# Six output tiles and a query GEMM around the second norm, one tile behind the first turn, and first passes on a constant

## The chip, the cores and the metric

The kernel runs on one core of a Trainium2 chip. The metric is the device time of one execution in microseconds (us), median of three.

## What is computed

One block of a hybrid network on 256 tokens of width 1024, all in float32. A mixer (a sparse attention of 8 heads and a gated recurrence of 4 heads) ends in the product with w_out; then come a residual and a layer norm. A cross attention of 4 heads over 256 memory rows ends in the product with xa_wo; then the second residual and norm. Last come product-key experts: a query for 8 heads, the best 16 of 128 by 128 keys for each, a product of all tokens with the 16384 rows of down, a gelu, the gates, and a product with the 16384 rows of up; then the third residual and norm. Cut to what matters here:

```python
mix = _hybrid_mixer(x, ...)                       # ends in @ w_out
x = _layer_norm(DEEPNORM_ALPHA * x + mix, ln_g[l, 0], ln_b[l, 0])
xa = _memory_cross_attention(x, mem, ...)         # ends in o @ wo
x = _layer_norm(DEEPNORM_ALPHA * x + xa, ln_g[l, 1], ln_b[l, 1])
qry = (t @ wq).reshape(T, PEER_HEADS, 2, PEER_DKEY // 2)
s = jnp.einsum('thcd,hcnd->thcn', qry, sub_keys)
s1, i1 = lax.top_k(s[:, :, 0], PEER_TOPK)
```

## The kernel before

All large weights come as a stream of tiles of 128 by 1024 numbers (512 KB), loaded by SP's queue into eight raw slots, for the expert tables into five. Every product is made at near float32 precision with two rounded numbers per operand: ACT copies a raw tile into `hi` (`split`, L600), DVE or, for tiles POOL_FROM to POOL_TO, POOL subtracts it from the raw tile into `lo`, in the raw tile's place (`rest`, L800; POOL's at L586), and PE makes three products (`three`, L1254 to L1256): hi by hi, hi by lo, lo by hi. There are four `hi` slots, so tile n + 4 is split when tile n is used (semaphore tile_used).

Tiles have two kinds. A column tile (T) holds 128 output columns for all 1024 input rows: 8 blocks of k, 24 products of 256 columns, and the result stands transposed, feature by token. A row tile (R) of width 512 holds two blocks of k: 6 products of 512 columns for each of two token tiles of 128 tokens (t = 0 and 1), 12 in all, and the result stands token by feature. A matrix of 1024 columns is 8 tiles of either kind. `plan` (L49) lists them, `order` (L126) writes one list, ORDER, of steps by hand, and every engine walks it and does its own part of each step, in order. The names that matter:

- `gemm`: PE's products with a tile; ACT takes a finished column result out of psG and splits tile n + 4, DVE makes the remainder. `feed` and `feed_lo` are the split and the remainder alone.
- `joint`: the last three output tiles, all of them for t = 0 first and then for t = 1, so that the norm of t = 0 can begin.
- `norm`: DVE adds the residual (`add_residual`, L817), takes the statistics, and normalizes in two halves of 512 columns (`normalize`, L832 and L838); ACT takes the root (L751).
- `turn`: PE transposes 128 tokens (L1549), ACT copies the result rounded into o_hi or b_hi (L757), DVE the remainder into o_lo or b_lo (`turn_lo`, L1125). Turns 0 and 1 are of the recurrence's output (four transposes each, ahead of the third tile of w_out, and `gemm` waits for o_lo at its first product), turns 2 and 3 of the first norm, 4 and 5 of the second, for t = 0 and 1.
- `route`: PE scores one head of the query against the keys, two products (L1526), ACT copies the scores out (L742), and DVE searches (`route`, L955 to L986): 8-wide maxima, index searches, replacements, and a sum of all 16 by 16 pairs (L967).

Around the second norm ORDER is: the cross attention's stages with ten stream tiles between them (the last two are output tiles), three more output tiles, `joint` of three, the norm of t = 0 and t = 1, turns 4 and 5, and then the eight column tiles of the query, a `route` behind each from the second on. Then the down table begins, a column tile for every 128 experts (`down`); DVE, which is then still searching, makes remainders again from table tile 24 on.

At the start SP loads x in four parts and tile 0 in two halves between them, then tiles 1, 2 and 3 whole; ACT splits x (L684) and tile 0 (L688) by parts, DVE makes the remainders (L936, L941), and PE's first product waits for them.

## Time and profile before

| | |
|---|---|
| median of 3 runs | 1080.71 us (1078.92 to 1081.68) |
| the profiled execution | 1080.01 us, span 1077.9 us |
| PE busy | 1051.9 us (98%) |
| DVE, ACT, POOL busy | 765.5, 513.5, 83.8 us |
| mean granted TensorE clock | 0.993 |

The profile shows one execution: for each engine its instructions with start and duration, what an idle time ended with, and the clock granted to TensorE in a stretch. Products are pipelined, so their pace is read from start to start, not from the duration of one. "Idle before" with an arrow names the instruction that released the engine.

### The profile page before, as it was taken

The page shows a single profiled execution, that of the slowest core. Times are in us where ns is not written, and L with a number is a line of the kernel's source. Part 1 is how long each engine was busy: PE and PEld are TensorE (multiplying, and loading weights), DVE is VectorE, ACT ScalarE, POOL GpSimd, SP SyncE. Part 2 cuts the span into 40 slices and gives each one's busy share as a digit, 9 for nine tenths or more (in the row PEclk, how much of TensorE's full clock was granted, in tenths as well). Part 3 has the DMA queues.
Part 4 walks back from the last instruction along what each step waited for, and adds up shares of the span by engine and source line. Part 5 has one row for each costly group of instructions (what it writes and reads, how often), then busy time and mean ns, then how long its engine had stood idle before and what let it go on. Part 6 is the DMA issues. An engine that isn't in the chain of part 4 may idle for free.

```text
span 1077.9 us, 18835 instructions
## 1 busy us (share of the span) xinstructions
PE 1051.9 (98%) x7648; PEld 949.2 (88%) x7648; DVE 765.5 (71%) x1431; ACT 513.5 (48%) x806; POOL 83.8 (8%) x57
## 2 busy tenths in 40 slices
PE   7999999999899999999999999999999999999996
PEld 6987887898799999999999999988888888888885
DVE  4667766845799876446888885488889885555556
ACT  5554544454455555544444444544444444554542
POOL 3000000000268700000000000000000000000000
PEclk9999999999899999999999999999999999999999
DMA  9843234643335555555544545565555555665652
GB/s 328 338 163 98 99 118 135 240 136 118 98 118 177 185 187 178 179 187 176 163 157 159 169 162 176 177 215 176 176 169 170 173 173 195 195 192 190 191 192 94
DMA packets 51589, 186.61 MB, mean 173 GB/s; under 512 B 5936, under 2 KB 5984, under 8 KB 51120
## 3 DMA queue, kind: packets, MB, share of 16 engines
q1 hardware_dynamic: 49680, 178.80, 50.7%
q0 software_dynamic: 1824, 6.61, 1.8%
q8 instruction: 61, 1.00, 0.4%
q14 instruction: 24, 0.20, 0.1%
HBM read 183.82 MB, written 1.05 MB: 172 GB/s over the span
## 4 chain that ended last, share of the span: by engine, by line
PE 95%; DVE 3%; DMA 1%; ACT 1%; issue 0%; SPq 0%; ACTq 0%
PE psG L1254 17%; PE psG L1255 17%; PE psG L1256 17%; PE psS L1606 16%; PE psT L1606 16%; PE psO L1574 2%; PE psO L1575 1%; PE psO L1501 1%; DMA raw<-in_w_stream 1%; PE psS L1413 1%; PE psO L1436 1%; PE psS L1357 1%; DVE x L838 1%; PE psS L1254 1%; PE psS L1256 1%; PE psS L1255 1%
## 5 line engine op out<-in xcount | busy, mean ns | idle before, releaser
L800 DVE TENSOR_TENSOR lo<-raw,hi 128x1024 fp32r<-128x1024 f32 x302 | 368.3, 1221 | 152.7 <-ACT hi L600 152.6
L600 ACT ACTIVATE hi<-raw 128x1024 fp32r<-128x1024 f32 x330 | 349.1, 1059 | 264.9 <-DMA raw<-in_up 188.1
L1254 PE MATMUL psG<-b_hi,hi 128*128 128x256 f32 x1152 | 332.2, 288 | 1.6 <-DVE b_lo L1125 1.2
L1255 PE MATMUL psG<-b_lo,hi 128*128 128x256 f32 x1152 | 327.2, 284 | 0.0
L1256 PE MATMUL psG<-b_hi,lo 128*128 128x256 f32 x1152 | 327.1, 284 | 0.0
L1254 PEld LDWEIGHTS psG<-b_hi,hi 128*128 128x128 f32 x1152 | 222.3, 193 | 3.7 <-issue 3.4
L1255 PEld LDWEIGHTS psG<-b_lo,hi 128*128 128x128 f32 x1152 | 222.4, 193 | 0.2
L1256 PEld LDWEIGHTS psG<-b_hi,lo 128*128 128x128 f32 x1152 | 222.2, 193 | 0.0
L766 ACT ACTIVATE H<-psG 128x256 f32<-128x256 f32 x128 | 49.1, 383 | 174.5 <-PE psG L1256 174.5
L1232 DVE TENSOR_TENSOR act_lo<-H,act_hi 128x256 fp32r<-128x256 f32 x128 | 54.0, 424 | 98.2 <-ACT act_hi L784 98.0
L1606 PE MATMUL psS<-hi,act_hi 128*128 128x512 f32 x248 | 79.5, 401 | 0.0
L586 POOL TENSOR_TENSOR lo<-raw,hi 128x1024 fp32r<-128x1024 f32 x28 | 69.6, 2491 | 97.3 <-ACT hi L600 97.3
L1606 PE MATMUL psT<-lo,act_hi 128*128 128x512 f32 x248 | 76.8, 391 | 0.0
L1606 PE MATMUL psT<-hi,act_hi 128*128 128x512 f32 x248 | 76.8, 391 | 0.0
L1606 PE MATMUL psS<-lo,act_hi 128*128 128x512 f32 x248 | 76.7, 391 | 0.0
L1606 PE MATMUL psS<-hi,act_lo 128*128 128x512 f32 x248 | 76.6, 390 | 0.0
L1606 PE MATMUL psT<-hi,act_lo 128*128 128x512 f32 x248 | 76.6, 390 | 0.0
L1254 PE MATMUL psG<-o_hi,hi 128*128 128x256 f32 x192 | 57.5, 300 | 8.1 <-DVE lo L941 7.2
L1255 PE MATMUL psG<-o_lo,hi 128*128 128x256 f32 x192 | 55.7, 290 | 0.0
L1256 PE MATMUL psG<-o_hi,lo 128*128 128x256 f32 x192 | 55.6, 290 | 0.0
L1606 PEld LDWEIGHTS psT<-hi,act_lo 128*128 128x128 f32 x248 | 46.6, 188 | 10.1
L1606 PEld LDWEIGHTS psT<-lo,act_hi 128*128 128x128 f32 x248 | 46.6, 188 | 10.1
(320 smaller groups left out, 1439.7 us busy)
## 6 DMA issues: line engine op xcount, KB each, us to landing
raw<-in_down SPq DMA_DIRECT2D x128, 512.0 KB, 3.5
raw<-in_up SPq DMA_DIRECT2D x128, 512.0 KB, 3.5
raw<-in_w_stream SPq DMA_DIRECT2D x74, 512.0 KB, 3.6
w<-in_w SPq DMA_DIRECT2D x4, 512.0 KB, 11.5
xT<-in_xT SPq DMA_DIRECT2D x4, 256.0 KB, 5.6
memT<-in_memT SPq DMA_DIRECT2D x1, 1024.0 KB, 8.1
x_tok<-in_x_tok POOLq DMA_DIRECT2D x1, 1024.0 KB, 8.6
ln_gb<-in_ln_g POOLq DMA_DIRECT2D x2, 512.0 KB, 6.9
```

Of the source, the lines that this page charges most:

```text
L586: pool.tensor_tensor(lo[slot(n)][:], raw[slot(n)][:], hi[n % DEPTH][:].bitcast(FP32), ALU.subtract)\
L600: act.activation(hi[n % DEPTH][:], raw[slot(n)][:], ACT.Copy).then_inc(hi_done, 1)
L766: act.activation(H[:, j, :], psG[j % 2][:, 0:S], ACT.Gelu).then_inc(h_out, 1)
L800: dve.tensor_tensor(lo[slot(n)][:], raw[slot(n)][:], hi[n % DEPTH][:].bitcast(FP32), ALU.subtract)\
L838: dve.scalar_tensor_tensor(out=z[:, half], in0=z[:, half], scalar=rs[:, t, 0:1], in1=gb[:, 1, half], op0=ALU.mult, op1=ALU.add).then_inc(r ...
L1232: dve.tensor_tensor(a_lo[j % 4][:], H[:, j, :], a_hi[j % 4][:].bitcast(FP32), ALU.subtract)\
L1254: pe.matmul(out, hi_l, hi_r, start=start, stop=False)
L1255: pe.matmul(out, hi_l, lo_r, start=False, stop=False)
L1256: return pe.matmul(out, lo_l, hi_r, start=False, stop=stop)
L1357: pe.matmul(psS[:, at:at + keys], qT[group * HD:(group + 1) * HD, 2 * g + j, t * P:(t + 1) * P], kT[b][group * HD:(group + 1) * HD, 0:keys ...
L1574: pe.matmul(out[:, k, :], one2[s][:, k // 2, :, k % 2], one1_hi[s][:, k // 2, :, k % 2], start=True, stop=False)
L1606: mm = pe.matmul((psS, psT)[t][:, c * 512:(c + 1) * 512], left[:, cut], right[:, c * 512:(c + 1) * 512], start=st, stop=False)
```

## The change

- **The start.** DVE sets a small bf16 array to one, and PE makes 28 products of 256 columns with it (WARM) into psT, whose result nothing reads, before the first real product. Tile 1 is loaded, split and subtracted in two halves, as tile 0 is.
- **The first turn.** The tiles of w_out come in another order: (0, 0), (0, 2), then the first tile of the second half (1, 0), then (0, 4), (0, 6) and the joint three. The turns stand ahead of the third tile as before, which is now (1, 0). Turns 0 and 1 write to psG, turns 2 and 5 to psT, 3 and 4 to psO.
- **The second norm.** Six output tiles (CROSS_JOINT) are made for t = 0 first; then four of them for t = 1, turn 4, and the other two for t = 1. The query of the first four heads is made of four row tiles, for t = 0 ahead of turn 5 and for t = 1 behind it. ACT copies its two banks to `probs`, PE transposes them (8 transposes) to psT, and ACT copies them to qryT. Four column tiles for the other heads follow, with one, two, two and three `route` steps behind them.
- **Slots.** Output and query tiles also use four more `hi` slots in the place of o_hi and o_lo, which are free by then. POOL makes the remainders from the third query tile on (before, from the fifth).

```diff
-        ("xo", "R", 0, 2), ("pq", "T", 0, KD)]
...
-CROSS_TILES = [(0, 0), (1, 0), (0, 2), (0, 4), (0, 6), (1, 2), (1, 4), (1, 6)]
-JOINT = 3
+        ("xo", "R", 0, 2), ("pq", "R", 0, 1), ("pq", "T", 4, 4)]
...
+OUTPUT_TILES = {"wo": [(0, 0), (0, 2), (1, 0), (0, 4), (0, 6), (1, 2), (1, 4), (1, 6)],
+                "xo": [(0, 0), (1, 0), (0, 2), (0, 4), (0, 6), (1, 2), (1, 4), (1, 6)]}
+JOINT, CROSS_JOINT = 3, 6
...
+FIRST, WARM = 2, 28
...
-    gemm(AT["pq"] - JOINT - n)
-    joint = range(n, n + JOINT)
-    n += JOINT
-    out += [("joint", joint[0]), ("norm", (1, 0))] + [("feed", m) for m in joint]
-    out += [("norm", (1, 1)), ("turn", 4), ("turn", 5), ("turn_lo", 4), ("turn_lo", 5)] + [("feed_lo", m) for m in joint]
+    assert n == AT["pq"] - CROSS_JOINT
+    joint = range(n, n + CROSS_JOINT)
+    n += CROSS_JOINT
+    out += [("part", (m, 0)) for m in joint]
+    out += [("feed", m) for m in joint[:4]] + [("feed_lo", m) for m in joint[:4]] + [("norm", (1, 0))]
+    out += [("part", (m, 1)) for m in joint[:4]] + [("feed", m) for m in joint[4:]]
+    out += [("turn", 4), ("half", 1), ("turn_lo", 4)] + [("part", (m, 1)) for m in joint[4:]]
+    query = range(n, n + 4)
+    n += 4
+    out += [("feed", query[0]), ("feed", query[1]), ("norm", (1, 1))] + [("part", (m, 0)) for m in query]
+    out += [("turn", 5), ("turn_lo", 5), ("query", 0), ("feed", query[2]), ("feed", query[3])]
+    out += [("part", (m, 1)) for m in query] + [("query", 1), ("turn_query", 0), ("turn_query", 1)]
     gemm(1)
-    for h in range(PH):
-        gemm(min(1, N1 - n))
-        out.append(("route", h))
+    out += [("route", 0)]
+    gemm(1)
+    out += [("route", 1), ("route", 2)]
+    gemm(1)
+    out += [("route", 3), ("route", 4)]
+    gemm(1)
+    out += [("route", h) for h in range(5, PH)]
     return out
...
-POOL_FROM, POOL_TO = N1 - 4, N1 + 24
+POOL_FROM, POOL_TO = N1 - 6, N1 + 24
...
+def hi_slot(n):
+
+    q = (n - AT["xo"]) % (2 * DEPTH)
+    if AT["xo"] <= n < N1 and q >= DEPTH:
+        return q
+    return n % DEPTH
...
+        held[hi_slot(n)] = n
...
+        o_at = place["at"]
         o_hi = sb("o_hi", [P, KD, S], F32R)
         o_lo = sb("o_lo", [P, KD, S], F32R)
+        hi += [sb(f"hi{DEPTH + i}", [P, D], F32R, at=o_at + i * D * 4) for i in range(DEPTH)]
         ln_gb = sb("ln_gb", [P, 2, D])
...
+        warm_in = sb("warm_in", [P, S], BF16, at=place["at"])
...
+        def turned_out(i, b):
+
+            return psG[i][:] if i < 2 else turned_bank(i)[:, b * 512:(b + 1) * 512]
+
+        def turned_bank(i):
+
+            return psT if i in (2, 5) else psO
...
-            for n in range(1, ALL):
+            for n in range(1, FIRST):
+                for c in range(2):
+                    half = slice(c * D // 2, (c + 1) * D // 2)
+                    sp.dma_start(raw[n][:, half], a["w_stream"][n][:, half]).then_inc(first_in[2 * n + c], 16)
+            for n in range(FIRST, ALL):
...
+                elif what == "query":
+                    if i == 0:
+                        act.wait_ge(query_done, 1)
+                        act.wait_ge(cross_turned, XH)
+                    else:
+                        act.wait_ge(tile_used, AT["pq"] + 4)
+                    act.activation(probs[:, i * 512:(i + 1) * 512], bank[BANK[TILES[AT["pq"]][8] + i]], ACT.Copy)\
+                        .then_inc(act_took, 1)
+                elif what == "turn_query":
+                    act.wait_ge(query_turned, i + 1)
+                    act.activation(qryT[:, 0:4, i * P:(i + 1) * P],
+                                   psT[:, i * 512:(i + 1) * 512].rearrange("p (k c) -> p k c", c=P), ACT.Copy)\
+                        .then_inc(query_ready, 1)
...
+            dve.memset(warm_in[:], 1.0).then_inc(warm_ready, 1)
...
+            for n in range(1, FIRST):
+                for c in range(2):
+                    half = slice(c * D // 2, (c + 1) * D // 2)
+                    dve.wait_ge((first_hi, hi_done)[c], n + 1)
+                    dve.tensor_tensor(lo[n][:, half], raw[n][:, half], hi[n][:, half].bitcast(FP32), ALU.subtract)\
+                        .then_inc((first_lo, lo_done)[c], 1)
...
+                elif what == "half":
+                    add_residual(FIRST_HALVES[2], (i,))
                 elif what == "norm":
                     w, t = i
-                    add_residual((AT["wo"] + KD, AT["pq"])[w] - 1, (t,))
+                    for n in FIRST_HALVES[2 * w:2 * w + 2]:
+                        if n >= (AT["wo"] + KD, AT["pq"])[w] - (JOINT, CROSS_JOINT)[w] and (w, t, n) != (1, 1, FIRST_HALVES[2]):
+                            add_residual(n, (t,))
...
+            def part(n, t):
+
+                name, kind, i, k0, m, cols, first, last, use = TILES[n]
+                lo_wait(n)
+                if name == "xo":
+                    pe.wait_ge(cross_lo, k0 // 2 + 1)
+                if name == "pq" and k0 % 4 == 0:
+                    pe.wait_ge(turn_lo, TURNED[4 + t] - 1 + k0 // 4)
+                if name == "pq" and k0 == 0:
+                    pe.wait_ge(dve_took, TAKEN[BEFORE[use + t]][1])
+                for kk in range(m):
+                    cut = slice(kk * cols, (kk + 1) * cols)
+                    k = k0 + kk
+                    left_hi, left_lo = (o_hi, o_lo) if name == "wo" else (b_hi, b_lo)
+                    mm = three(bank[BANK[use + t]], left_hi[:, k, t * P:(t + 1) * P],
+                               left_lo[:, k, t * P:(t + 1) * P], hi[hi_slot(n)][:, cut], lo[slot(n)][:, cut],
+                               k == 0, k == KD - 1)
+                if t == NT - 1:
+                    mm.then_inc(tile_used, 1)
+                elif last:
+                    mm.then_inc(query_done if name == "pq" else first_half, 1)
...
+            pe.wait_ge(warm_ready, 1)
+            for i in range(WARM):
+                pe.matmul(psT[:, 0:S], warm_in[:, 0:P], warm_in[:], start=True, stop=True)
             for what, i in ORDER:
                 if what in ("gemm", "bare"):
                     gemm(i)
                 elif what == "joint":
-                    joint(i)
+                    for t in range(NT):
+                        for m in range(i, i + JOINT):
+                            part(m, t)
+                elif what == "part":
+                    part(*i)
+                elif what == "turn_query":
+                    pe.wait_ge(act_took, TAKEN[TILES[AT["pq"]][8] + i][1])
+                    pe.wait_ge(turn_lo, TURNED[5])
+                    for h in range(4):
+                        mm = pe.transpose(psT[:, i * 512 + h * P:i * 512 + (h + 1) * P],
+                                          probs[:, i * 512 + h * P:i * 512 + (h + 1) * P], ident[:])
+                    mm.then_inc(query_turned, 1)
...
-                    pe.wait_ge(act_took, TAKEN[TILES[AT["pq"] + i][8]][1])
+                    if i < 4:
+                        pe.wait_ge(query_ready, NT)
+                    else:
+                        pe.wait_ge(act_took, TAKEN[TILES[AT["pq"] + i][8]][1])
...
                     if i == 0:
-                        pe.wait_ge(exp_done, XU)
-                        pe.wait_ge(probsT_ready, XU)
+                        pe.wait_ge(act_took, TAKEN[TILES[AT["mv"]][8] + 1][1])
                     elif i in (2, 3):
...
                         if i < 2:
-                            src = oh[:, t, k % 4 * P:(k % 4 + 1) * P]
+                            src, out = oh[:, t, k % 4 * P:(k % 4 + 1) * P], psG[t][:, k % 4 * P:(k % 4 + 1) * P]
                         else:
                             src = (x1, x2)[i // 2 - 1][:, t, k * P:(k + 1) * P]
-                        mm = pe.transpose((psO if i in (2, 4) else (psS, psT)[t])[:, k * P:(k + 1) * P], src, ident[:])
+                            out = turned_bank(i)[:, k * P:(k + 1) * P]
+                        mm = pe.transpose(out, src, ident[:])
                         if k % 4 == 3:
```

How the order moves. PE at the first turn, of the kernel before (`oh` is the recurrence's output, `p_hi` and `o_hi` the left operands of w_out's first and later rows, psO and psS the banks of its first and second half):

```order
L1256 MATMUL psO<-hi_54,o_lo 128x512
L1549 MATMUL psS<-ident,oh 128x128 x4
L1549 MATMUL psT<-ident,oh 128x128 x4
L1254 MATMUL psO<-hi_55,o_hi 128x512
L1255 MATMUL psO<-lo_61,o_hi 128x512
```

and of the change:

```order
L1333 MATMUL psO<-lo_59,o_hi 128x512
L1334 MATMUL psO<-hi_54,o_lo 128x512
L1648 MATMUL psG<-ident,oh 128x128 x8
L1332 MATMUL psS<-hi_55,p_hi 128x512
L1333 MATMUL psS<-lo_61,p_hi 128x512
L1334 MATMUL psS<-hi_55,p_lo 128x512
```

Behind the transposes stood products with o_hi, which the turn writes; now 12 products with p_hi and p_lo stand there first. ACT at the second norm, of the kernel before (from the root of t = 0 to the first query result; `hi` from `raw` is a split):

```order
L751 ACTIVATE std<-mv 128x1
L600 ACTIVATE hi_54<-raw_66 128x1024
L600 ACTIVATE hi_55<-raw_107 128x1024
L600 ACTIVATE hi_56<-raw_109 128x1024
L751 ACTIVATE std<-mv 128x1
L757 ACTIVATE b_hi<-psO 128x4x128 x2
L757 ACTIVATE b_hi<-psT 128x4x128 x2
L617 ACTIVATE qryT<-psG 128x256
```

and of the change:

```order
L820 ACTIVATE std<-mv 128x1
L653 ACTIVATE hi_55<-raw_107 128x1024
L653 ACTIVATE hi_56<-raw_109 128x1024
L826 ACTIVATE b_hi<-psO 128x4x128 x2
L653 ACTIVATE hi_115<-raw_111 128x1024
L653 ACTIVATE hi_116<-raw_58 128x1024
L820 ACTIVATE std<-mv 128x1
L826 ACTIVATE b_hi<-psT 128x4x128 x2
L787 ACTIVATE probs<-psG 128x512
L653 ACTIVATE hi_117<-raw_60 128x1024
L653 ACTIVATE hi_118<-raw_62 128x1024
L787 ACTIVATE probs<-psG 128x512
```

Both turns stood behind both roots; now turn 4 stands between them, with two splits ahead of it, and two more splits stand ahead of the root of t = 1.

## Rows read from the trace of the kernel before

**Rows 1.** page, section 1, the whole span
```profile
PE 1051.9 (98%) x7648; PEld 949.2 (88%) x7648; DVE 765.5 (71%) x1431; ACT 513.5 (48%) x806; POOL 83.8 (8%) x57
```

**Rows 2.** what PE waited for, whole span: us in total, times, longest
```profile
PE psG L1254 <- DVE lo L941: 7.2, 2, 6.6
...
PE psT L1549 <- DVE x L838: 3.4, 2, 2.6
...
PE psO L1254 <- DVE o_lo L1125: 2.3, 1, 2.3
...
PE psG L1254 <- DVE b_lo L1125: 1.2, 1, 1.2
```

**Rows 3.** busy time by stretch, granted TensorE clock last but two
```profile
0.00:15.40 15.40, 8.01 (x33) 7.20 (x34) 6.98 (x9) 8.39 (x11) 5.48 (x13) 1.00 0.84 303
...
179.00:182.60 3.60, 3.60 (x10) 2.81 (x9) 0.13 (x1) 0.00 (x0) 0.00 (x0) 0.53 0.00 0
...
279.50:285.00 5.50, 5.48 (x26) 5.50 (x27) 3.87 (x4) 0.00 (x0) 0.00 (x0) 0.50 0.00 0
```

**Rows 4.** order of time, the first tiles: start us, us, engine, instruction [idle before]
```profile
12.27 3.77 DVE L800 TENSOR_TENSOR lo<-raw,hi 128x1024 fp32r<-128x1024 f32 x3 [1.34 <-ACT hi L600]
...
12.45 1.06 ACT L600 ACTIVATE hi<-raw 128x1024 fp32r<-128x1024 f32 x1 [0.22 <-DMA raw<-in_w_stream]
...
13.55 0.58 PE L1254 MATMUL psG<-o_hi,hi 128*128 128x256 f32 x1 [0.24 <-DVE lo L800]
...
14.78 0.41 PE L1256 MATMUL psG<-o_hi,lo 128*128 128x256 f32 x1
...
14.99 0.41 PE L1254 MATMUL psG<-o_hi,hi 128*128 128x256 f32 x1
...
15.51 0.28 PE L1254 MATMUL psG<-o_hi,hi 128*128 128x256 f32 x1
...
15.63 0.28 PE L1255 MATMUL psG<-o_lo,hi 128*128 128x256 f32 x1
```

**Rows 5.** order of time, PE after the first turn
```profile
179.66 0.63 PE L1254 MATMUL psO<-hi,o_hi 128*128 128x512 f32 x1
...
180.08 0.63 PE L1255 MATMUL psO<-lo,o_hi 128*128 128x512 f32 x1
```

**Rows 6.** order of time, PE and DVE at the second norm
```profile
271.23 0.39 PE L1254 MATMUL psS<-hi,b_hi 128*128 128x512 f32 x1
...
271.46 0.39 PE L1255 MATMUL psS<-lo,b_hi 128*128 128x512 f32 x1
...
272.77 0.68 DVE L817 SCALAR_TENSOR_TENSOR x<-x,psS 128x512 f32<-128x512 f32 x1
...
277.63 0.66 PE L1549 MATMUL psT<-ident,x 128*128 128x128 f32 x4 [0.80 <-DVE x L838]
```

**Rows 7.** page, sections 5 and 6: POOL's remainders, loads of the stream
```profile
L586 POOL TENSOR_TENSOR lo<-raw,hi 128x1024 fp32r<-128x1024 f32 x28 | 69.6, 2491 | 97.3 <-ACT hi L600 97.3
...
raw<-in_w_stream SPq DMA_DIRECT2D x74, 512.0 KB, 3.6
```

**Rows 8.** the stream's loads in the first 20 us
```profile
DMA to landing us min/median/max: 7.6/11.5/16.6
```

**Rows 9.** order of time, scoring, search and tile 24
```profile
287.74 1.03 PE L1526 MATMUL psO<-subk,qryT 128*128 128x256 f32 x4
...
289.92 1.06 DVE L955 MAX8 unit_m<-route_s 128x8 f32<-128x128 f32 x4 [6.54 <-ACT route_s L742]
...
311.72 0.47 PE L1254 MATMUL psG<-b_hi,hi 128*128 128x256 f32 x1
...
343.03 2.58 DVE L967 TENSOR_TENSOR unit_c<-unit_m 128x256 f32<-128x256 f32 x2
...
353.88 0.74 DVE L967 TENSOR_TENSOR unit_c<-unit_m 128x256 f32<-128x256 f32 x2
...
374.35 1.34 DVE L800 TENSOR_TENSOR lo<-raw,hi 128x1024 fp32r<-128x1024 f32 x1 [2.01 <-ACT hi L600]
```

More of the change, by code:

```diff
@@ L245, with hi_slots @@
 SLOT_BEFORE, ARRIVED = slots()
+def hi_slot(n):
[3 more added lines that the diff above has]
+    return n % DEPTH
+def hi_slots():
+    held, before = {q: AT["xo"] - 1 for q in range(DEPTH, 2 * DEPTH)}, []
+    for n in range(ALL):
+        before.append(held.get(hi_slot(n)))
+        held[hi_slot(n)] = n
+    return before
+HI_BEFORE = hi_slots()
 def table_order():
@@ L466, in build @@
         x_in = [sem(f"x_in{i}") for i in range(4)]
-        first_in = [sem(f"first_in{i}") for i in range(2)]
+        first_in = [sem(f"first_in{i}") for i in range(2 * FIRST)]
+        warm_ready = sem("warm_ready")
         first_hi, first_lo = sem("first_hi"), sem("first_lo")
@@ L597, in split @@
                 act.wait_ge(raw_in[slot(n)], ARRIVED[n])
[L598 to L600 removed]
+                if HI_BEFORE[n] is not None:
+                    act.wait_ge(tile_used, HI_BEFORE[n] + 1)
+                act.activation(hi[hi_slot(n)][:], raw[slot(n)][:], ACT.Copy).then_inc(hi_done, 1)
             def take(n):
@@ L689, in _ @@
                         .then_inc((first_hi, hi_done)[i // 2], 1)
-            for n in range(1, DEPTH):
+            for n in range(1, FIRST):
+                for c in range(2):
+                    half = slice(c * D // 2, (c + 1) * D // 2)
+                    act.wait_ge(first_in[2 * n + c], 16)
+                    act.activation(hi[n][:, half], raw[n][:, half], ACT.Copy).then_inc((first_hi, hi_done)[c], 1)
+            for n in range(FIRST, DEPTH):
                 split(n)
```

78 lines of the change are left out of this document (31 added, 47 removed).

## The prediction

> **What bounds the kernel now.** I read first the busy shares: PE is busy for 98% of the span [rows 1], so only what lengthens or empties PE counts: its idle time, and passes that take longer than they need. The list of PE's waits came second. Four entries hold 14.1 of PE's idle time [rows 2]: 7.2 us for the first remainders of the weights, 3.4 us for normalized rows and 1.2 us for b_lo (both at the second norm), 2.3 us for o_lo at the first turn. Third I looked at the pace of the products. With 256 columns they follow each other by 0.12 us, but until 15.4 us by 0.21 us [rows 4]; with 512 columns by 0.227 us [rows 6], but behind the first turn by 0.42 us [rows 5]. The granted clock explains it: 0.53 in 179.0 to 182.6 us and 0.50 in 279.5 to 285.0 us, the level of 1.2 GHz in place of 2.4 [rows 3]. Each time PE had run a few transposes and waited before. For the first 15.4 us the column shows 1.00, but the step of 0.21 us is that of the 1.2 GHz stretches; there I go by the step. So three places cost PE twice, by a wait and by a slow clock behind it, and the change touches exactly these three. Last comes what lies behind: the search for experts on DVE, between 289.92 us and the remainder of table tile 24 at 374.35 us [rows 9], without a pause.
>
> **The start.** Added: a memset on DVE, 28 passes of 256 columns on a constant, and halves for tile 1 (one load, one ACT and one DVE instruction more, each of half size). At the slow step the passes take 28 x 0.213 = 6.0 us; PE is otherwise idle until 6.6 us [rows 2], so begun near 1 us they end near 7.0 us at worst. No trace shows bf16 passes here, so I bound them: at 0.12 us each they are over by 4.4 us, and if each took the 0.41 us that a slow one lasts in the rows [rows 4], they would end at 12.5 us and push the rest. I take the step of the fp32r passes with as many columns. What is won is read at tile 2: before, tile 1 starts at 13.55 us, makes 8 products at 0.21 and 16 at 0.12 us, and tile 2 starts at 17.2 us. With the fast level all along, tiles 0 and 1 no longer bound: the raw data of tile 2 arrive at 12.45 us, ACT takes 1.06 us, DVE 1.26 us (a third of 3.77) [rows 4], so tile 2 starts at 14.8 to 15.0 us. Gain 2.2 us; bounds 2.4 (nothing but that chain) and minus 1.1 (passes of 0.41 us). The halves of tile 1 alone, at a slow clock, give 0.5 us, since tile 1 then follows tile 0 without the pause before 13.55 us. Later tiles had slack: PE does not wait for a tile between 15.4 us and the turn, so the gain stays.
>
> **The first turn.** The output tile (1, 0) of 12 products, 12 x 0.227 = 2.7 us, comes between the transposes and the tile that needs o_lo. It uses only p_hi, p_lo and a weight tile already split; the transposes go to psG, which ACT has emptied by then. ACT and DVE do the same work in the same order behind the transposes, so o_lo is ready as before, 2.3 us behind them, and 2.7 us cover it. The wait of 2.3 us goes [rows 2]; the 3.6 us at a granted 0.53 [rows 3] shrink by 1.7 us, if the clock stays up while PE works. Gain 4.0 us. What moves: the residual of the first half comes one tile later on DVE, 2.7 us of work beside 4.1 us of joint products (18 x 0.227); it stays hidden. Bounds: 2.3 (the clock falls all the same) and 4.0.
>
> **The second norm.** On PE's own clock of before, the last six output tiles start at 271.9 - 72 x 0.227 = 255.6 us, and all their products for token tile 0 are done at 263.8 us in place of 267.8 us. DVE needs 5.0 us from there to the last normalized half (272.77 us is where it took up token tile 1 behind it [rows 6]), so x2 is ready near 268.8 us, while PE works on token tile 1 until 269.2 us. The turn of token tile 0 thus needs no wait. Behind it PE has 12 products (2.7 us) before the query GEMM, which covers ACT's and DVE's copies. But ACT now stands with two weight splits ahead of these copies, whose loads are issued only when parts for token tile 1 have freed slots, at 265 and 266.5 us; with 3.6 us to landing [rows 7] the second split ends at 271.1 us, b_lo at 272.6 us, PE arrives at 272.8 us: just covered. Then 24 products on token tile 0 (5.4 us, to 278.2 us) hide the norm of token tile 1, which DVE ends at 278.0 us. Only the turn of token tile 1 is open: before, its last transposes (0.66 us [rows 6]) and the wait for b_lo (1.2 us [rows 2]) took 1.9 us together; now eight transposes (1.0 us) run in these 1.9 us, which leaves 0.9 to 1.0 us idle. So of 3.4 + 1.2 us and a further 0.4 us at the first transposes, 1.0 remains: 4.0 us won. A new wait of 0.35 us arises between the two transposed query banks (a copy of 512 columns on ACT), and 8 transposes cost 1.0 us. Four query tiles as 48 products of 0.227 us in place of 96 of 0.12 us save 0.6 us. The stretch of 5.5 us at 0.50 [rows 3] becomes 3.0 us if the clock holds: 2.4 us (25 products at 0.213 in place of 0.12). Scoring comes in pairs behind column tiles, so PE changes between kinds of product five times in place of nine, 0.5 us. Together 4.0 - 0.35 - 1.0 + 0.6 + 2.4 + 0.5 = 6.2 us. Bounds: 3.8 (clock falls in the one idle place) and 7.2 (the turn needs no wait).
>
> **What is late next.** The search on DVE does not move as far as PE. Counted as above, token tile 1 of the query ends at 285.6 us, the transposed queries are there at 286.9 us, and the first column tile ends at 290.0 us in place of 287.74 us; the search follows by 2.2 us [rows 9]. It starts 2.3 us later, while PE's table tiles start 6.2 us earlier. Before, DVE was free 2.0 us before its remainder of tile 24 (374.35 us less the 2.01 us that it waited) and could have had it by 373.7 us; PE needs it at 311.72 + 24 x 2.88 + 0.2 = 381.0 us. The slack of 7.3 us meets a shift of 8.5 us: PE waits 1.2 us. Tiles before 24, and two query tiles more than before, come from POOL at 2.49 us each [rows 7] against 2.88 us of PE; that holds. Sum: 2.2 + 4.0 + 6.2 - 1.2 = **11.2 us** off the profiled 1080.0 us, 1068.8 us. The median of the runs shown is 0.7 us above that execution: **1069.5 us**.
>
> **Rivals.** (a) The first passes lose the fast level again, because PE has little to do between 7 and 10.4 us; for it speaks that idle stretches of 2 to 3 us ended in a slow clock twice [rows 3], against it that these pauses are shorter. The start gives 0.5 us, the time is 1071.2 us. Chance 0.17. (b) The search takes longer. A pair of sums at L967 takes 0.74 us or, beside a POOL subtraction, 2.58 us [rows 9]; over the eight heads such delays make 5.0 us. If five more of the eight were caught, at 1.84 us each 9.2 us, PE would wait 10.4 us: 1078.7 us; with two more, 1073.2 us. Chance of at least one and a half more 0.17. The Trainium skill ("SBUF — State Buffer", section "Who interferes with whom") says that a DVE instruction with two SBUF inputs and a GpSimd instruction reading SBUF exclude each other for a whole instruction; by that rule all eight pairs can be caught, and the search would be longer by 8 x 1.84 - 5.0 = 9.7 us in place of the unchanged length that I take. The trace agrees in the two lengths of the pair. (c) On the other side, slower: the loads behind the six tiles land late, and ACT, which works in order, holds the copies of the turn behind them. At 3.6 us to landing it costs nothing; each us above is a us of PE's wait at the query GEMM, and a slow stretch of 2.4 us follows. In the first 20 us, with many loads queued, landing took 7.6 to 16.6 us [rows 8]. At 11.5 us the loss is 10.3 us, which leaves 2.1 of 12.4 us (DVE is late as well, so tile 24 then costs nothing), 1078.6 us; slower than before from 13.6 us on, and 1083.7 us at 16.6 us. Against it: here only the weight stream loads. Chance 0.03. (d) The clock falls behind the turns all the same: 2.2 + 2.3 + 3.8 = 8.3 us, tile 24 then without a wait, 1072.4 us; the same that (a) has for and against it holds here. Chance 0.10.
>
> **How the numbers follow.** The forecast keeps 0.53. The range of 1066.8 to 1074.0 us runs from no wait at tile 24 and a little more from the turn, through (a), (d) and the nearer part of (b); the far part of (b) and (c) are left out. 0.3% is 3.2 us, about what a measurement of this kernel can tell from no change; faster than 1077.5 us are the forecast, (a), (d) and most of (b): 0.93. Within 0.3%: the far end of (b) and the mild case of (c), 0.05. Slower: 0.02.
>
> **What would show it.** Right: products 0.12 us apart from about 7 us on, tile 2 near 15 us; no wait for o_lo; the one wait behind the last turn near 1 us; no stretch at a granted 0.5 near either norm; table tile 0 starting near 299.3 us; one PE wait of about 1 us for DVE's lo near 368 us, since the search then ends last. Wrong: a slow step between 7 and 15 us (a); a wait of several us at tile 24 (b); PE waiting for b_lo before the query GEMM, with ACT waiting for the stream's loads (c).

## The result and the profile after

| | before | changed |
|---|---|---|
| median, same chip | 1080.69 us (4 runs) | 1073.44 us (4 runs: 1072.74 to 1077.50) |
| ratio of the times | 1 | 0.9949, 95% interval 0.9930 to 0.9969 |
| the profiled execution | 1080.01 us, span 1077.9 | 1077.50 us, span 1075.2 |

The change is faster, but by half of what was forecast: 0.51% by the ratio, 5.5 us of 1080 (by the interval 3.3 to 7.6), where 11.2 us were worked out. The two medians, of four runs each, lie 7.3 us apart; in the longer series of the same kernel (e1_after, below: five runs beside eleven) they lie 5.2 us apart, with a ratio of 0.9947 (0.9934 to 0.9960). What follows goes by the ratios. The profiled execution happens to be the slowest of the four; the second profile shows what is common to both.

First the page and PE's waits, as in [rows 1] and [rows 2] (us in total, times, longest). The change shifts line numbers: L1332 to L1334 are the products now, L653 the split, L668 `take`, L868 the remainder, L885 the residual, L900 and L906 the two normalize instructions, L1042 the search's sums of pairs, L1200 `turn_lo`, L1648 the transposes (one more each where the order list grew by a line, as in e2_pool).

```profile
PE 1054.6 (98%) x7636; PEld 947.6 (88%) x7636; DVE 762.6 (71%) x1431; ACT 514.1 (48%) x807; POOL 88.6 (8%) x59
```

```profile
PE psG L1332 <- ACT qT L668: 3.1, 2, 2.5
...
PE psT L1648 <- DVE x L906: 2.4, 2, 1.6
...
PE psG L1332 <- DVE lo L1010: 1.4, 1, 1.4
```

The wait for o_lo is gone, as forecast. The waits for `lo` fell from 7.2 to 1.4 us; 6.1 us of that stretch are now the constant passes, which are counted as busy. A new one stands on top: 3.1 us for ACT's copy of a finished product (qT), and the wait for normalized rows only fell from 3.4 to 2.4 us.

Busy time by stretch; the granted clock is the last column but two [rows 3]:

```profile
0.00:15.40 15.40, 12.48 (x76) 10.21 (x76) 7.23 (x11) 8.71 (x12) 5.47 (x13) 1.00 0.85 301
...
31.00:34.40 3.40, 3.40 (x19) 3.40 (x18) 2.26 (x2) 1.27 (x3) 0.00 (x0) 0.51 0.69 276
...
178.00:204.00 26.00, 26.00 (x125) 21.67 (x123) 20.98 (x31) 11.66 (x15) 0.65 (x2) 1.00 0.56 178
...
280.20:283.70 3.50, 3.44 (x10) 2.89 (x11) 1.31 (x2) 2.29 (x4) 0.18 (x1) 0.51 0.00 0
```

Nothing slow is left between the first turns and turn 3. But two stretches run low, and neither is in the forecast's sum: one behind the new wait for qT, one behind turn 5 (part of rival (d)).

The start, in order of time (start us, us, engine, instruction [idle before]), to be read with [rows 4]:

```profile
1.19 6.14 PE L1525 MATMUL psT<-warm_in 128*128 128x256 bf16 x28 [1.19 <-DVE warm_in L1001]
...
7.00 0.45 PE L1332 MATMUL psG<-o_hi,hi 128*128 128x256 f32 x1
...
15.50 0.35 PE L1332 MATMUL psG<-o_hi,hi 128*128 128x256 f32 x1 [0.39 <-ACT kvc L668]
...
28.27 1.06 ACT L653 ACTIVATE hi<-raw 128x1024 fp32r<-128x1024 f32 x1 [5.47 <-DMA raw<-in_w_stream]
...
29.23 0.36 ACT L668 ACTIVATE qT<-psG 128x256 f32<-128x256 f32 x1
...
29.74 0.36 PE L1332 MATMUL psG<-o_hi,hi 128*128 128x256 f32 x1 [2.50 <-ACT qT L668]
```

The constant passes end where forecast, the first real product follows at 7.00 us, and tile 2 starts at 15.50 us (before: 17.30). So 1.8 us were won by then. Then ACT stands 5.5 us for the load of tile 7. Its copy of tile 4's result is queued behind that split, and PE, which needs the bank, waits 2.5 us and from 31 us runs slow for 3 us. The transposes of turns 0 and 1 begin at 177.84 us; before, at 175.36.

The second norm, to be read with [rows 6]:

```profile
267.50 1.04 PE L1648 MATMUL psO<-ident,x 128*128 128x128 f32 x8
...
268.32 9.88 POOL L639 TENSOR_TENSOR lo<-raw,hi 128x1024 fp32r<-128x1024 f32 x4 [62.34 <-ACT hi L653]
...
270.73 1.29 DVE L1200 TENSOR_TENSOR b_lo<-psO,b_hi 128x512 fp32r<-128x512 f32 x2 [2.33 <-ACT b_hi L826]
...
271.93 0.68 DVE L885 SCALAR_TENSOR_TENSOR x<-x,psS 128x512 f32<-128x512 f32 x1
...
273.69 2.29 DVE L900 SCALAR_TENSOR_TENSOR x<-x,mv,ln_gb 128x512 f32<-128x512 f32 x1
...
276.08 2.67 DVE L906 SCALAR_TENSOR_TENSOR x<-x,rstd,ln_gb 128x512 f32<-128x512 f32 x1
...
278.68 0.74 DVE L900 SCALAR_TENSOR_TENSOR x<-x,mv,ln_gb 128x512 f32<-128x512 f32 x1
...
278.81 0.66 PE L1648 MATMUL psT<-ident,x 128*128 128x128 f32 x4 [1.58 <-DVE x L906]
...
281.60 0.63 PE L1333 MATMUL psG<-lo,b_hi 128*128 128x512 f32 x1
...
282.02 0.63 PE L1334 MATMUL psG<-hi,b_lo 128*128 128x512 f32 x1
```

Turn 4 comes without a wait. POOL begins on a query tile's remainder at 268.32 us and makes four in one go, to 278.20. While it runs, DVE's first two normalize instructions of token tile 1 (L900, L906) last 2.29 and 2.67 us, the third, behind it, 0.74. Beside POOL, too, but with one operand from PSUM, b_lo (two in 1.29 us) and the residual (0.68) take no longer than in the kernel before, where no POOL instruction ran beside them. Turn 5 then waits, and products of 512 columns follow by 0.42 us.

The search, to be read with [rows 9]:

```profile
292.04 1.03 PE L1625 MATMUL psO<-subk,qryT 128*128 128x256 f32 x4
...
294.22 1.07 DVE L1030 MAX8 unit_m<-route_s 128x8 f32<-128x128 f32 x4 [11.49 <-ACT route_s L811]
...
307.68 0.47 PE L1332 MATMUL psG<-b_hi,hi 128*128 128x256 f32 x1
...
372.11 2.36 DVE L868 TENSOR_TENSOR lo<-raw,hi 128x1024 fp32r<-128x1024 f32 x2
```

Down tile 0 starts at 307.68 us, 4.0 us earlier than before, not 12.4. DVE is through with the search and at the table's remainders by 372.11 us, where it waits for nothing; nor does PE wait at down tile 24. The search, from its first maximum to the table's first remainder, takes 77.9 us; before it took 82.4 (from 289.92 us until DVE was free at 372.34).

### The profile page after: what moved, and what is told of

Read it like the earlier page. It is cut to its first block, busy times and chain, and to the rows that moved or that the text cites. A ratio compares the mean times of both kernels' runs of the same rounds, so it can differ in the third digit from the quotient of the medians.

```text
span 1075.2 us, 18826 instructions
## 1 busy us (share of the span) xinstructions
PE 1054.6 (98%) x7636; PEld 947.6 (88%) x7636; DVE 762.6 (71%) x1431; ACT 514.1 (48%) x807; POOL 88.6 (8%) x59
## 4 chain that ended last, share of the span: by engine, by line
PE 92%; DMA 3%; DVE 2%; ACT 1%; SPq 1%; issue 1%
PE psG L1332 16%; PE psS L1705 16%; PE psG L1333 16%; PE psG L1334 16%; PE psT L1705 16%; DMA raw<-in_w_stream 2%; PE psO L1673 2%; PE psO L1674 1%; PE psO L1597 1%; PE psS L1495 1%; PE psO L1518 1%; PE psS L1439 1%; DVE x L906 1%; PE psS L1332 1%; PE psS L1333 1%
## 5 line engine op out<-in xcount | busy, mean ns | idle before, releaser
L653 ACT ACTIVATE hi<-raw 128x1024 fp32r<-128x1024 f32 x329 | 347.8, 1059 | 267.2 <-DMA raw<-in_up 190.4
L868 DVE TENSOR_TENSOR lo<-raw,hi 128x1024 fp32r<-128x1024 f32 x299 | 364.1, 1220 | 140.6 <-ACT hi L653 140.2
L1332 PE MATMUL psG<-b_hi,hi 128*128 128x256 f32 x1120 | 321.2, 287 | 0.7 <-ACT hg_t L681 0.4
L1333 PE MATMUL psG<-b_lo,hi 128*128 128x256 f32 x1120 | 316.8, 283 | 0.0
L1334 PE MATMUL psG<-b_hi,lo 128*128 128x256 f32 x1120 | 316.8, 283 | 0.0
L1332 PEld LDWEIGHTS psG<-b_hi,hi 128*128 128x128 f32 x1120 | 214.8, 192 | 2.6 <-issue 2.5
L1333 PEld LDWEIGHTS psG<-b_lo,hi 128*128 128x128 f32 x1120 | 214.9, 192 | 0.1
L1334 PEld LDWEIGHTS psG<-b_hi,lo 128*128 128x128 f32 x1120 | 214.8, 192 | 0.0
L639 POOL TENSOR_TENSOR lo<-raw,hi 128x1024 fp32r<-128x1024 f32 x30 | 74.4, 2490 | 89.9 <-ACT hi L653 89.8
L1332 PE MATMUL psG<-o_hi,hi 128*128 128x256 f32 x192 | 56.7, 295 | 5.1 <-ACT qT L668 2.5
L1705 PEld LDWEIGHTS psS<-lo,act_hi 128*128 128x128 f32 x248 | 46.5, 188 | 10.1
L1705 PEld LDWEIGHTS psS<-hi,act_lo 128*128 128x128 f32 x248 | 46.5, 188 | 10.1
```

The lines of the kernel that those rows point to most:

```text
L639: pool.tensor_tensor(lo[slot(n)][:], raw[slot(n)][:], hi[hi_slot(n)][:].bitcast(FP32), ALU.subtract)\
L653: act.activation(hi[hi_slot(n)][:], raw[slot(n)][:], ACT.Copy).then_inc(hi_done, 1)
L868: dve.tensor_tensor(lo[slot(n)][:], raw[slot(n)][:], hi[hi_slot(n)][:].bitcast(FP32), ALU.subtract)\
L1332: pe.matmul(out, hi_l, hi_r, start=start, stop=False)
L1333: pe.matmul(out, hi_l, lo_r, start=False, stop=False)
L1334: return pe.matmul(out, lo_l, hi_r, start=False, stop=stop)
```

## The experiments

All times are medians, and each ratio is taken beside the kernel before on the same chip. The chips differ: the kernel before has medians of 1078.9 to 1081.1 us on them. So times are compared within the groups that ran on one chip (e1 to e4_w1; e4b, e4c, e5_both and e6; e5b, e7 and e8), and across groups by the ratios. Most of what follows is read from five legs of PE's way, in one profiled execution of each kernel, each leg from the start of one instruction to that of the next: to the transposes of turns 0 and 1; to turn 3; to down tile 0; to the first gate product; to the last product.

| kernel | to turn 0 | to turn 3 | to down 0 | to gates | to the end | time, us | ratio (95%) |
|---|---|---|---|---|---|---|---|
| before | 175.4 | 30.5 | 105.8 | 188.0 | 568.7 | | |
| changed | 177.8 | 26.3 | 103.5 | 188.5 | 569.5 | 1073.4 | 0.9949 (0.9930-0.9969) |
| e1_after | 176.4 | 26.3 | 102.2 | 188.5 | 569.4 | 1073.7 | 0.9947 (0.9934-0.9960) |
| e2_pool | 176.1 | 26.3 | 101.1 | 188.1 | 568.6 | 1072.7 | 0.9943 (0.9930-0.9956) |
| e3_oldstart | 176.5 | 26.3 | 102.5 | 188.1 | 569.4 | 1075.3 | 0.9958 (0.9945-0.9972) |
| e4_w1 | 173.5 | 26.3 | 102.1 | 189.7 | 570.1 | 1073.4 | 0.9942 (0.9927-0.9957) |
| e4b_w1_nowarm | 174.8 | 26.3 | 103.6 | 188.6 | 568.7 | 1073.5 | 0.9941 (0.9929-0.9954) |
| e4c_w1_old | 175.1 | 26.3 | 102.1 | 188.8 | 569.5 | 1074.1 | 0.9947 (0.9933-0.9960) |
| e5_both | 173.8 | 26.3 | 100.4 | 188.6 | 569.4 | 1070.1 | 0.9909 (0.9894-0.9923) |
| e5b_both | 173.6 | 26.3 | 100.4 | 188.0 | 568.8 | 1069.9 | 0.9902 (0.9884-0.9920) |
| e6_turn | 174.7 | 30.5 | 103.5 | 188.5 | 569.4 | 1078.4 | 0.9982 (0.9969-0.9995) |
| e7_to | 174.4 | 26.3 | 101.3 | 188.0 | 568.8 | 1069.9 | 0.9898 (0.9880-0.9916) |
| e8_order | 173.3 | 26.3 | 101.6 | 188.8 | 568.9 | 1070.0 | 0.9901 (0.9883-0.9919) |
| e10_feed | 173.7 | 26.3 | 99.8 | 188.4 | 570.0 | 1069.6 | 0.9898 (0.9879-0.9916) |

**The changed kernel again.**

> The changed kernel once more, nothing edited, for a second profile and a firmer ratio. Its first profile was its slowest execution (1077.5 us where the others took 1072.7 to 1073.5), with a TensorE stretch at the low clock between 31 and 34 us behind a 2.5 us wait for tile 7's load. If the others lack that stretch, this profile has turn 1's transposes near 174 us and not at 177.8, and the time is near 1073.4; if the start is as in the first profile in every execution, they stand at 177.8 and the time is 1077. The second norm is to look the same as in the first profile: the first two normalize instructions of token tile 1 at 2.3 and 2.7 us where 0.74 is their alone time, turn 5 with 1.6 and 0.8 us of waits, and the low clock behind it.

```profile
28.31 1.06 ACT L653 ACTIVATE hi<-raw 128x1024 fp32r<-128x1024 f32 x1 [3.94 <-DMA raw<-in_w_stream]
...
272.56 1.99 DVE L900 SCALAR_TENSOR_TENSOR x<-x,mv,ln_gb 128x512 f32<-128x512 f32 x1
...
274.67 2.68 DVE L906 SCALAR_TENSOR_TENSOR x<-x,rstd,ln_gb 128x512 f32<-128x512 f32 x1
```

Turn 0 stands at 176.40 us and not at 174: tile 7 is split at 28.31 us here too, and PE waits 2.2 us for it; only the slow stretch behind it is missing. DVE's two instructions are slow again (1.99 and 2.68 us). So both flaws belong to the kernel; the slow stretches behind them are in the first profile and not in this one.

**DVE makes the query tiles' remainders.**

```diff
-POOL_FROM, POOL_TO = N1 - 6, N1 + 24
+POOL_FROM, POOL_TO = N1, N1 + 24
-("turn", 4), ("half", 1), ("turn_lo", 4)
+("turn", 4), ("half", 1), ("feed_lo", joint[4]), ("turn_lo", 4), ("feed_lo", joint[5])
 ("turn", 5), ("turn_lo", 5), ("query", 0), ("feed", query[2]), ("feed", query[3])
+[("feed_lo", m) for m in query]
```

> GpSimd starts its remainders with down tile 0; VectorE makes those of the six query tiles (one ahead of the turn's remainders, one behind, four behind turn 5, where it stood idle). Theory 1: GpSimd's subtractions took VectorE's normalize of token tile 1 from 0.74 to 2.3 and 2.7 us, and what TensorE lost at turn 5 was 4.5 us between its last product of token tile 0 and the sixth of token tile 1 (6.6 us, where eight transposes and six products at full clock take 2.2), of which some 1.2 us of turn, copy and remainder stay. It expects both instructions at 0.75 us, turn 5 without a wait, and 3.3 us less than the changed kernel: 1070.1. Theory 2: the lost part of the gain sits elsewhere (start, search), and the norm is bound by the chain of copies and remainders: within 1 us of the changed kernel. Theory 3: the six added subtractions on VectorE (1.2 us each) make the search or b_lo late: slower than the changed kernel by up to 2 us.

```profile
270.96 1.22 DVE L869 TENSOR_TENSOR lo<-raw,hi 128x1024 fp32r<-128x1024 f32 x1
...
273.85 0.74 DVE L901 SCALAR_TENSOR_TENSOR x<-x,mv,ln_gb 128x512 f32<-128x512 f32 x1
...
274.70 0.75 DVE L907 SCALAR_TENSOR_TENSOR x<-x,rstd,ln_gb 128x512 f32<-128x512 f32 x1
...
276.12 0.60 PE L1649 MATMUL psT<-ident,x 128*128 128x128 f32 x4
...
276.96 0.66 PE L1649 MATMUL psT<-ident,x 128*128 128x128 f32 x4 [0.24 <-DVE x L907]
...
278.18 0.47 PE L1333 MATMUL psG<-hi,b_hi 128*128 128x512 f32 x1 [0.56 <-issue]
```

Although DVE makes two remainders ahead of it, the norm is done earlier: the two instructions take 0.74 and 0.75 us, and turn 5 waits 0.24 us between its halves and no more. The leg to down tile 0 is 1.1 us shorter than in e1_after. Over the kernels of the table with the leg as in the change (seven, mean 102.8 us) and those with DVE making the remainders (e2, e5, e5b, e7, mean 100.8 us) it is 2.0 us. Theory 1 holds as to the mechanism, with 2 us where 3.3 were expected: the 4.5 us were counted in the first profile, which also had the slow clock there. The time alone (1072.7 beside 1073.7) would not have decided it; e4_w1 and e5_both below, which differ in this edit, do: ratios of 0.9942 and 0.9909, with intervals that do not meet.

**The old start.** In the changed kernel `FIRST, WARM = 2, 28` becomes `1, 0`.

> The changed kernel with the start of the kernel before: tile 1 in one piece, no passes on a constant. Forecast's term: the start is worth 2.2 us, so 2.2 us slower than the changed kernel, 1075.6. Theory from the first profile of the changed kernel: the start is swallowed, since from tile 3 on ScalarE waits for every load of the stream, and the loads are no earlier: 0 to 1 us slower. If the first profile is the typical one, it is 2.5 us faster (1071).

Turn 0 stands at 176.5 us, within 0.1 us of e1_after. Over all profiles with w1's loads in the old place, the new start has 177.8, 176.4, 176.1 and 174.7 (mean 176.3), the old one 175.4 and 176.5 (mean 175.9). So by the turn no gain of the start is left in the profiles, which are few and scatter by 3 us. The time is 1.6 us longer than e1_after's, nearer to the forecast's term than to the theory's middle, with executions of the two kernels overlapping (1072.9 to 1075.6; 1072.9 to 1074.6). What the start is worth in this order of the loads stays open, between nothing and some 1.6 us.

**w1's loads later.**

```diff
-                if 3 <= n < 7:
-                    kv, part = (n - 3) // 2, ...
+                if 7 <= n < 11:
+                    kv, part = (n - 7) // 2, ...
```

> The changed kernel with the four 512 KB loads of w1 issued behind tiles 7 to 10 and not behind tiles 3 to 6 of the same queue. Theory 1: the first 28 us are bound by the loads (a tile every 2.5 us from tile 4 on, since a load of w1 stands between any two), and tile 7, for which ScalarE and behind it TensorE waited, comes 5 us earlier; TensorE then has no wait at tile 6 and keeps its clock: turn 1 at 174 us or below, and 1 to 2 us less than the changed kernel's median, more against an execution like its first profile. Theory 2: the queue moves the same bytes by 45 us in either order, w1 comes late for its products at 44 us, and the wait only moves: no change, or slower by up to 2 us.

Splits of tiles 5 and 6 on ACT, a pair of sums of DVE's search, and PE's wait at down tile 24:

```profile
16.41 1.06 ACT L653 ACTIVATE hi<-raw 128x1024 fp32r<-128x1024 f32 x1
...
18.75 1.05 ACT L653 ACTIVATE hi<-raw 128x1024 fp32r<-128x1024 f32 x1
...
361.32 3.87 DVE L1042 TENSOR_TENSOR unit_c<-unit_m 128x256 f32<-128x256 f32 x2
...
PE psG L1332 <- DVE lo L868: 0.8, 1, 0.8
```

Tile 5 is split at 16.41 us where it was at 18.99, and from tile 6 on ACT waits for no load. Turn 0 comes at 173.46 us. In six profiles with this order and the new start it is 173.3 to 174.4, mean 173.7; so the order of the loads is worth 2.5 us at the turn, and the scatter falls from 3 us to 1. w1 is not late. Yet the time hardly moves in this pair (1073.4 beside 1073.7, where 1 to 2 us less were expected): the search on DVE now ends last, one of its pairs of sums lasts 3.87 us, PE waits 0.8 us for it, and the leg behind takes back 1.2 us. In time the edit shows on top of e2_pool's: a ratio of 0.9943 (0.9930 to 0.9956) without it, 0.9909 (0.9894 to 0.9923) with it, in e5_both.

**What of the start is the start's.** Both with w1 late: without the constant passes (`WARM = 0`), and with all of the old start.

> The kernel with w1's loads behind tiles 7 to 10 (e4_w1), and the 28 passes on a constant left out; tile 1 stays in two pieces. In e4_w1 the start was kept: turn 1's transposes at 173.5 us, 2.9 before the changed kernel's 176.4. Theory 1: the passes hold TensorE's clock over the first products; without them the products from 7 us on run at the low level, as in the kernel before, and the transposes stand 0.5 to 1.5 us later, 174.0 to 175.0. Theory 2: the first tiles wait for loads anyway, and the passes are worth nothing: 173.5.

> The kernel with w1's loads behind tiles 7 to 10, and the whole start of the kernel before (tile 1 in one piece, no constant). Theory 1: the start is worth what the forecast put down, 2.2 us, but only where no later load is waited for; turn 1's transposes at 175.7, 2.2 behind e4_w1's 173.5. Theory 2: the start is worth nothing in either order of the loads (e3_oldstart stood at 176.5 beside 176.4 of the changed kernel), and all 2.9 us of e4_w1 are the loads': 173.5 here too.

Without the passes the first products have the slow step until 15.4 us, as before (that kernel in order of time: two slow products in a row, and two fast ones):

```profile
14.75 0.41 PE L1332 MATMUL psG<-o_hi,hi 128*128 128x256 f32 x1
...
14.96 0.41 PE L1333 MATMUL psG<-o_lo,hi 128*128 128x256 f32 x1
...
15.71 0.28 PE L1332 MATMUL psG<-o_hi,hi 128*128 128x256 f32 x1
...
15.83 0.28 PE L1333 MATMUL psG<-o_lo,hi 128*128 128x256 f32 x1
```

Turn 0 comes 1.1 us later than with them (174.8 beside the mean of 173.7), and 1.3 us later with the old start. Each of the two is one profile, but both lie above all six with the passes. So theory 1 is right in kind in both, and the whole start is worth about 1.3 us at the turn where no later load is waited for; 2.2 were forecast. The times (1073.5 and 1074.1 us, and e4_w1's 1073.4 on another chip) are too near each other to tell.

**The order of the first output tiles undone.**

```diff
-"wo": [(0, 0), (0, 2), (1, 0), (0, 4), (0, 6), (1, 2), (1, 4), (1, 6)]
+"wo": [(0, 0), (0, 2), (0, 4), (0, 6), (1, 0), (1, 2), (1, 4), (1, 6)]
```

> The changed kernel with the order of the first output tiles undone: the third tile behind turn 1 is again the one that needs the turned rows. Forecast's term: the order is worth 4.0 us; the profiles have 26.3 us from turn 1 to turn 3 where the kernel before had 30.5. So 30.4 here, and 4 us slower than the changed kernel, 1077.7. Rival: part of it was idle time that tile 24 gives back (VectorE's search is later by the same 4 us, so is TensorE, and nothing is to be given back): 3 us or less.

```profile
PE psO L1332 <- DVE o_lo L1200: 2.3, 1, 2.3
```

The old wait is back, and so is the slow stretch behind it:

```profile
178.80:182.20 3.40, 3.40 (x10) 2.63 (x9) 0.00 (x0) 0.00 (x0) 0.00 (x0) 0.50 0.00 0
```

The leg is 30.5 us again, 4.2 us more. The time is 1078.4 us; by the ratios (0.9982 where the change has 0.9949 and 0.9947) it rises by 3.6 to 3.8 us. This one line is the largest part of the gain.

**Both repairs together**, e2_pool's and e4_w1's edits, and a second time:

> e2_pool and e4_w1 together: VectorE makes the six query tiles' remainders, w1 behind tiles 7 to 10. If both parts stand on their own, the profile has turn 1 at 173.3, turn 3 to down tile 0 in 101.1 us (102.2 in the changed kernel), down tile 0 at 300.7, and the last product 2.9 + 1.1 us before the changed kernel's less what the search on VectorE takes back at down tile 24 (1.2 us in e4_w1): 1059 us, a time of 1070 to 1071. Rival: the search ends last at tile 24 and takes all of it from e4_w1 on: last product at 1060.5, no better than e2_pool.

> e5_both once more, unedited, as the base of the two runs beside it: 1070.1 us, ratio 0.991, last product near 1058.6.

1070.1 and 1069.9 us, ratios 0.9909 and 0.9902: some 10 us below the kernel before, where the change is 5.5 below. The legs come out as expected, and the search takes back 0.5 us in one profile and nothing in the other.

**Three small edits on top of it.** POOL makes down tiles 24 and 25 too (`POOL_TO = N1 + 26`):

> e5_both with GpSimd making two more remainders (down tiles 24 and 25). In e5_both 188.6 us lie between the first product of down tile 0 and the first gate product; the least that any profile showed is 188.0, with the search not ending last. Theory: the search ends last at tile 24 and costs 0.6 us there; 188.0 here, 0.6 us less in all. Rival: two more subtractions of 2.4 us on GpSimd slow VectorE's work behind the search as they did the normalize: no gain, or up to 1 us slower.

188.0 us in that leg, the least there is, but e5b_both has 188.0 without the edit, and the time is the same to 0.1 us: no gain. The profile shows something else. Here the slow step came back behind the constant passes, though they ran as in the others:

```profile
13.30 0.41 PE L1333 MATMUL psG<-o_hi,hi 128*128 128x256 f32 x1
...
13.51 0.41 PE L1334 MATMUL psG<-o_lo,hi 128*128 128x256 f32 x1
```

The granted clock is 0.50 from 11.1 to 14.5 us, behind a wait of 1.4 us; tile 2 starts at 16.33 us and turn 0 at 174.4, the latest of the six. The nine other profiles with the passes have no such stretch before 31 us.

The last query tile of token tile 0 behind turn 5:

> e5_both with the products of the last query tile for token tile 0 behind turn 5 and not ahead of it, and VectorE's remainder of that tile behind the norm of token tile 1. In e5_both and e2_pool TensorE stands some 1.2 us between turn 5 and the first product of token tile 1: the turned rows' copy (0.6) and remainder (0.7) must come first. Six products (1.4 us) now lie in that gap. Worked out: turn 5 at once, 0.5 us of waiting for the tile's remainder, then no wait: 0.6 us less between turn 3 and down tile 0 (99.9 where e5_both had 100.4), 1069.5. Rival: a wait takes the place of the one removed (x not yet normalized when turn 5 begins 1.4 us earlier): no change.

```profile
268.03 0.47 PE L1333 MATMUL psG<-hi,b_hi 128*128 128x512 f32 x1 [1.25 <-issue]
...
273.30 0.66 PE L1649 MATMUL psT<-ident,x 128*128 128x128 f32 x4 [0.47 <-DVE x L907]
...
274.43 0.50 PE L1333 MATMUL psG<-hi,b_hi 128*128 128x512 f32 x1 [0.47 <-DVE lo L869]
```

The rival came: turn 5, which now stands six products (1.4 us) earlier in the order, waits 0.47 us for the second half of x, then PE waits 0.47 us for the tile's remainder. The first row is another gap, ahead of the query's first product; it is 0.9 us longer than e5_both's and makes most of what this leg is longer (101.6 us where 99.9 were expected).

That gap, in a last kernel, which rounds tile 70 behind turn 4's copies:

```diff
-[("feed", m) for m in joint[4:]], ("turn", 4), ("half", 1), ...
+("feed", joint[4]), ("turn", 4), ("feed", joint[5]), ("half", 1), ...
```

> e5_both with ScalarE's rounding of the sixth cross output's follower tile (tile 70) behind its two copies of turn 4, not ahead of them. In seven profiles TensorE stood 0.2 to 1.25 us ahead of the query's first product, and more the later tile 70's load landed (ScalarE's wait for it 0.92, 0.99, 1.21, 1.83, 2.04 us gave gaps of 0.23, 0.29, 0.55, 0.97, 1.17), since the copies stand behind that wait. Theory: the gap is at most 0.3 us now whatever the load does, and turn 3 to down tile 0 takes 100.0 to 100.4 us; no more than 0.3 us of time, 1069.7. Rival: the tile's remainder, now later, is missed by the query's last tile or holds the norm of token tile 1: turn 5 waits 1 us or more, 1071.

```profile
264.06 1.07 ACT L827 ACTIVATE b_hi<-psO 128x512 fp32r<-128x512 f32 x2
...
265.25 1.06 ACT L654 ACTIVATE hi<-raw 128x1024 fp32r<-128x1024 f32 x1
...
272.43 1.03 PE L1649 MATMUL psT<-ident,x 128*128 128x128 f32 x8
...
274.49 0.47 PE L1333 MATMUL psG<-hi,b_hi 128*128 128x512 f32 x1 [1.02 <-issue]
```

ACT copies the turn at once and splits the tile behind it; ahead of the query's first product PE no longer stands. The leg is 99.8 us, the shortest of all. The 1.02 us behind turn 5 are left. The time, 1069.6 us, can't be told from e5b_both's.

## Why the prediction was half right

**The sum.** By legs, the mean of the changed kernel's two profiles against the one of before: start -1.8, first turn +4.2, second norm +3.0 (105.8 less 102.8), search -0.5, rest -0.8; in all 4.2 us, where the ratio says 5.5. Both profiled executions were the slowest of their series (1077.5 and 1074.6 us, medians 1073.4 and 1073.7), and the start's leg scatters most: over the four profiles with this start and order of loads it is -0.9. The forecast had 2.2, 4.0, 6.2, -1.2 and 0. So two terms failed, the start and the second norm.

**The first turn** was right in mechanism and size: 4.0 forecast, 4.2 in the legs, 3.6 to 3.8 by e6_turn's ratio.

**The start** failed at its last sentence, "Later tiles had slack: PE does not wait for a tile between 15.4 us and the turn, so the gain stays." PE did not wait, but ACT did. In the kernel before it already stood for the loads of tiles 4 to 9, longest for tile 7, and the DMA engines' busy share from 20 to 30 us is 1.03; its split of tile 7, and that stretch (the DMA share is the last number but one):

```profile
25.92 1.06 ACT L600 ACTIVATE hi<-raw 128x1024 fp32r<-128x1024 f32 x1 [2.27 <-DMA raw<-in_w_stream]
...
20.00:30.00 10.00, 10.00 (x85) 10.00 (x85) 3.63 (x4) 4.38 (x7) 1.12 (x2) 1.00 1.03 342
```

The copy that PE needs for tile 6 stands behind that split. Of the kernel before, the copy and PE's first product of tile 6:

```profile
26.88 0.36 ACT L617 ACTIVATE qT<-psG 128x256 f32<-128x256 f32 x1
...
28.82 0.28 PE L1254 MATMUL psG<-o_hi,hi 128*128 128x256 f32 x1
```

The slack was thus some 1.4 us, less than the 1.8 us that PE gained. That alone would have cost about 0.4 us, an estimate from these rows. The larger part of the wait of 2.5 us is that tile 7 came later than before: split at 25.92 us there, at 26.60 to 28.31 us in the four profiles of the new start. Four loads of 512 KB that nobody needs before 44 us stood between PE's own; with them moved back (e4_w1) the wait is gone. With the old start and this order of the loads (the kernel before and e3_oldstart) tile 7 was split at 25.92 and 24.68 us, PE came to tile 6 at 28.82 and 29.96, and there is no such wait. Why tile 7 comes later behind the new start is open. What was read right is the first 15 us of this execution: passes over by 7.3 us, fast step at once, tile 2 at 15.5 us, 0.5 to 0.7 us behind the forecast, with a wait of 0.39 us for ACT's copy of the first result, which the forecast left out. The 17.2 us that the forecast took for tile 2 before was 17.3. Rival (a), a clock that falls again, came in one of ten profiles with the passes (e7_to); in the first profile the clock fell at 31 us, behind the wait that the loads made.

**The second norm** failed at two steps. The first is "which DVE ends at 278.0 us", with "two query tiles more than before, come from POOL at 2.49 us each against 2.88 us of PE; that holds". POOL was asked only whether it keeps up, not whom it slows. The mechanism stood in the prediction as rival (b), and was applied to the search alone; it struck the normalize of token tile 1, the one chain that PE waited for. By the Trainium skill ("SBUF — State Buffer", section "Who interferes with whom") a DVE instruction with two inputs in SBUF and a GpSimd instruction that reads SBUF exclude each other for a whole instruction. The trace agrees: the two normalize instructions last 2.29 and 2.67 us beside POOL's of 2.4 us (1.88 to 2.68 over the seven profiles in which POOL makes these remainders), the instructions there that read PSUM and SBUF 0.65 to 0.68 us. It cost 2.0 us in the leg. The second step is "just covered" for ACT's copies of turn 4 behind two splits. In the same seven profiles PE stood 0.17 to 0.98 us there, mean 0.5, more the later tile 70's load landed; in e10_feed it does not stand there. With both mended the leg is 99.8 us, 6.0 shorter than before, near the 6.2 worked out. The clock behind turn 5 fell in three of the seven (legs of 103.5, 103.6 and 103.5 us, the others 102.1 to 102.5): about 1.3 us in each, the second half of rival (d) in three of seven profiles.

**Behind it.** The forecast's wait of 1.2 us at down tile 24 took the search to be as long as before. In the changed kernel's two profiles it is 4 us shorter (77.9 and 78.4 us, before 82.4), and PE does not wait. Over the thirteen profiles, seven have a search of 81.7 to 82.4 us, and those seven have a wait for the remainder at tile 24, of 0.1 to 0.8 us (0.8 in e4_w1). In five it takes 77.9 to 78.4 us and there is no wait; in the sixth without one, e7_to, DVE has two tiles less to make. The sums of pairs go with it: 9.1 to 9.6 us in all where the search is short, 14.0 to 14.8 where it is long, 11.5 before. So where the search kept the length that the forecast gave it, the forecast's wait came, if a smaller one; rival (b), a search longer than before, came in none. Why an execution gets the one length or the other is open. The last 0.8 us lie at the end: in eight of the thirteen profiles PE waits some 0.5 us there for the last weight tile's remainder. The same kernel shows it in one profile (e5_both) and not in the other (e5b_both), so it is none of the change's.

**The chances.** Faster by over 0.3% was right. That 1073.4 us lies in the range, at its upper end, is in part luck: the range reached so far up for (a), (d) and the nearer part of (b) in the search, not for what took the gain. (a) to (d) were all about places that the change touches; that the gain at the start could vanish in a queue 15 us later was no case.

## What to carry to other kernels

Before an earlier start is counted as won, look at the engines that feed PE, not at PE: if the one that takes the loads already stands waiting for them, later stages have no slack, and what has to move is the queue's order; here three numbers of a condition gave 2.5 us at the first turn. When work is given to GpSimd, list what VectorE does in the same microseconds with two operands in SBUF: in these traces such an instruction of 0.74 us took up to 2.7 us beside GpSimd's of 2.4 us, and only those on PE's chain cost. On an engine that works through its list in order, put what PE waits for ahead of what waits for memory (e10_feed).
